# A hybrid decoder step on one core: the second chunk's first norm, the samples' pages and queries, the page-number check and the mixers' halves

## What is computed

```
x += 0.5 * SwiGLU1(RMSNorm(x))                      # 2816 hidden
z  = RMSNorm(x) @ w_in                              # q, k, v, indexer q/k/weights, conv B, C, h
       I[t,s] = sum_h w[t,h] relu(q_idx[t,h].k_idx[s]); keep top k = 256 keys (s <= t),
       softmax attention over the kept keys (8 q heads, 2 kv heads, dim 64, rotary)
       short gated conv (512 channels): y = B * conv_w3(C * h)
x += concat(attn, conv) @ w_out
x += 0.5 * SwiGLU2(RMSNorm(x))
x += sigmoid(RMSNorm(x) @ w_ple_gate) * (p @ w_ple_proj)
y  = RMSNorm(x)
```

## Time and profile before

| | before |
|---|---|
| median of 3 runs | 2928.32 us (2918.21 to 2932.49) |
| the profiled execution, its own time | 2924.44 us |
| its span, first to last instruction | 2922.7 us |
| mean granted TensorE clock | 0.943 |
| busy, share of the span | TensorE 89%, VectorE 45%, GpSimd 35%, ScalarE 34% |
| HBM | 89 GB/s over the span |

### The profile page before, as it was taken

How to read it: one execution, slowest core, us unless ns; L and a number is a source line. 1 busy time by engine, 2 the same in 40 slices (tenths; PEclk the granted TensorE clock), 3 DMA queues, 4 the chain that set the end, 5 groups by cost and what they waited for, 6 DMA issues and landing times.

```text
span 2922.7 us, 41456 instructions
## 1 busy us (share of the span) xinstructions
PE 2615.3 (89%) x15166; PEld 2282.7 (78%) x15166; DVE 1313.0 (45%) x3135; ACT 1001.1 (34%) x1625; POOL 1009.9 (35%) x521
## 2 busy tenths in 40 slices
PE   4999998998868888889898976888999999999997
PEld 4999997778646767777786676777889898778786
DVE  3223224438753333443365687766333232332344
ACT  3222223631213333335435311443444233332332
POOL 4333333232343333332244223212213344454440
PEclk9999998999878888899999988998999999999998
DMA  4333324221224343311222212111112223233212
GB/s 147 98 95 100 107 92 140 93 106 63 96 79 124 103 136 116 119 57 49 77 101 75 70 61 73 44 44 44 44 44 87 80 72 115 87 108 96 92 63 73
DMA packets 157038, 253.40 MB, mean 87 GB/s; under 512 B 15010, under 2 KB 101283, under 8 KB 156835
## 3 DMA queue, kind: packets, MB, share of 16 engines
q1 hardware_dynamic: 154144, 247.02, 26.5%
q10 hardware_dynamic: 2690, 3.72, 0.4%
HBM read 240.34 MB, written 18.73 MB: 89 GB/s over the span
## 4 chain that ended last, share of the span: by engine, by line
PE 69%; DVE 14%; ACT 4%; issue 4%; POOL 3%; DVEq 2%; DMA 1%; SPq 1%; ACTq 0%
PE ps L1442 21%; PE ps L1443 19%; PE ps L1444 19%; PE ps L1655 2%; PE ps L1711 2%; DVE hits L1242 1%; POOL w_lo L734 1%; DVE s_hits L1292 1%; DVE hits_late L1242 1%; PE ps L1641 1%; DVE ps L1092 1%; POOL d_lo L734 1%; PE ps L1577 1%; DVE ha_lo L1094 1%; SPq L613 1%
## 5 line engine op out<-in xcount | busy, mean ns | idle before, releaser
L734 POOL TENSOR_TENSOR w_lo<-raw,w_hi 128x1024 fp32r<-128x1024 f32 x250 | 602.5, 2412 | 1058.7 <-ACT w_hi L834 1058.1
L1442 PE MATMUL ps<-xna_hi,w_hi 128*128 128x288 f32 x2000 | 612.3, 306 | 29.6 <-DVE convf_a L1146 7.8
L1443 PE MATMUL ps<-xna_lo,w_hi 128*128 128x288 f32 x2000 | 600.7, 300 | 0.0
L1444 PE MATMUL ps<-xna_hi,w_lo 128*128 128x288 f32 x2000 | 599.8, 300 | 0.0
L1442 PEld LDWEIGHTS ps<-xna_hi,w_hi 128*128 128x128 f32 x2000 | 387.6, 194 | 44.6 <-issue 22.8
L1442 PE MATMUL ps<-xnb_hi,w_hi 128*128 128x512 f32 x1000 | 412.8, 413 | 0.3 <-DVE hb_lo L1094 0.3
L734 POOL TENSOR_TENSOR d_lo<-raw,d_hi 128x1024 fp32r<-128x1024 f32 x90 | 218.4, 2446 | 544.6 <-ACT d_hi L834 544.6
L1443 PE MATMUL ps<-xnb_lo,w_hi 128*128 128x512 f32 x1000 | 400.6, 401 | 0.0
L1444 PE MATMUL ps<-xnb_hi,w_lo 128*128 128x512 f32 x1000 | 400.2, 400 | 0.0
L1443 PEld LDWEIGHTS ps<-xna_lo,w_hi 128*128 128x128 f32 x2000 | 387.3, 194 | 0.2
L1444 PEld LDWEIGHTS ps<-xna_hi,w_lo 128*128 128x128 f32 x2000 | 386.5, 193 | 0.0
(11 more groups left out here) (291 smaller groups left out, 4126.8 us busy)
## 6 DMA issues: line engine op xcount, KB each, us to landing
raw<-in_w_gu SPq DMA_DIRECT2D x176, 512.0 KB, 3.5
raw<-in_w_d SPq DMA_DIRECT2D x88, 512.0 KB, 3.5
raw<-in_w_ring SPq DMA_DIRECT2D x74, 512.0 KB, 3.4
pages<-in_vk_pages SPq DMA_DIRECT2D x256, 128.0 KB, 2.7
idx_flat<-in_idx_pages SPq DMA_DIRECT2D x256, 32.0 KB, 2.1
idxp<-idx_flat SPq DMA_DIRECT2D x8, 1024.0 KB, 7.6
x_spill<-xa SPq DMA_DIRECT2D x1, 2304.0 KB, 8.9
xa<-x_spill SPq DMA_DIRECT2D x4, 576.0 KB, 5.9
```

The lines of the kernel that those rows point to most:

```text
L734: g_.tensor_tensor(lo[slot][:, :, :], raw[l % 2][:, :, :], hi[slot][:, :, :].bitcast(f32), ALU.subtract).then_inc(lo_done, 1)
L1442: mm(out, shi, mhi, start=first, stop=False)
L1443: mm(out, shi, mlo, start=False, stop=False)
L1444: return mm(out, slo, mhi, start=False, stop=last)
```

## The change

- **Start.** `weights` is cut in two: tiles 0 and 1 are split ahead of the first `sums`, tiles 2 and 3 behind the eight scales of chunk 0. Squares 0 to 3 of chunk 1 go between `sums` and `spread` of chunk 0, squares 4 to 7 between scales 3 and 4. `sums(0,1)` stands behind the first half of the first product, `spread(0,1)` and the scales of chunk 1 behind its second. The gathers are woven over a list shorter by these two parts.
- **Search and pages.** 10 search steps in the in-projection in place of 12, 22 in the feed-forward. The first three `kl` join the feed-forward's search groups 2, 4 and 6 (steps 12, 14, 16), `qs` and the first `ks` group 10 (step 20). SP's and GpSimd's wait for the mask becomes one for the in-projection's last product; ScalarE's is dropped. Search and choice steps are woven over parts 2 to 54 (2 to 50 before), the rest of the samples' work from part 55 (51). By the weave, the three choice steps then all follow the third down-projection (two of them preceded it), and four quarters lie between the last of them and the first `kq`.
- **Memory.** K pages move from FREE to XNA + 16384, the exponentials' input Sa from XNA to FREE, `above` and `cum` into the places of V pages 3 to 6; mask, scores and hits shift.
- **Page numbers** are loaded without the bounds check.
- **Mixers.** Copies and subtractions tile by tile, attn and conv alternately; TensorE waits per tile, SP for all.
- **End.** `spread(4,0)` behind the last product.

```diff
--- before.py
+++ after.py
@@ -231,9 +231,14 @@
         flat = lambda groups: [e for g in groups for e in g]
-        ev = [("begin",)] + flat(squares(0, 0)) + [("weights",)] + self.norm(0, 0) + flat(squares(0, 1)) + self.norm(0, 1)
+        scales = lambda k, c, ms: [("scale", k, c, m) for m in ms]
+        second = flat(squares(0, 1))
+        ev = [("begin",)] + flat(squares(0, 0)) + [("weights", 0), ("sums", 0, 0)] + second[:4] + [("spread", 0, 0)]
+        ev += scales(0, 0, range(4)) + second[4:] + scales(0, 0, range(4, KT)) + [("weights", 1)]
 
         first = self.two_chunks(0, range(FT))
+        ev += first[:1] + [("sums", 0, 1)] + first[1:2] + [("spread", 0, 1)] + scales(0, 1, range(KT))
+        first = first[2:]
         first = weave(first, [[("ga", i)] for i in range(NB * PAGES // 2)], 1, 140)
@@ -248,20 +253,24 @@
         side += [[("spread", 0, 2)] + [("scale", 0, 2, m) for m in range(4)], [("scale", 0, 2, m) for m in range(4, KT)], [("vtr", 0)]]
-        side += [[("st", j)] for j in range(12)]
+        side += [[("st", j)] for j in range(10)]
         ev += weave(first, side, 13, None)
         first = self.one_chunk(0)
-        search = [[("st", j)] for j in range(12, 32)] + [[("sties", i)] for i in range(3)] + [[("qs",)]]
+        search = [[("st", j)] for j in range(10, 32)] + [[("sties", i)] for i in range(3)]
         groups = self.samples()
+        for i in range(K_RING):
+            search[2 + 2 * i] += groups[i]
+        search[10] += [("qs",)] + groups[K_RING]
+        groups = groups[K_RING + 1:]
         for j in range(32):
-            groups[6 + 2 * j].append(("bt", "A", j))
+            groups[2 + 2 * j].append(("bt", "A", j))
         units = self.prompt(BLOCKS[0])
         units[6].append(("bties", 3))
-        first = weave(first, groups + units + [[], [("mix", 0)], [("back", 0)]], 51, -3)
-        ev += weave(first, search, 2, 50)
+        first = weave(first, groups + units + [[], [("mix", 0)], [("back", 0)]], 55, -2)
+        ev += weave(first, search, 2, 54)
         first = self.out_proj(0)
@@ -292,7 +301,7 @@
         end = len(first) - 4
-        ev += first[:end] + [("sums", 4, 0)] + first[end:end + 1] + [("spread", 4, 0)] + first[end + 1:]
+        ev += first[:end] + [("sums", 4, 0)] + first[end:] + [("spread", 4, 0)]
         ev += [("scale", 4, 0, m) for m in range(KT)] + [("y", 0)] + self.norm(4, 1) + [("y", 1)]
@@ -308,7 +317,7 @@
             if e[0] == "weights":
-                for w in range(RING):
+                for w in (2 * e[1], 2 * e[1] + 1):
                     split(("w", w), "w", w)
@@ -468,13 +477,13 @@
 
-        scores = {0: at("score0", [128, 128], f32, FREE + 12352), 1: at("score1", [128, 256], f32, FREE + 12864),
-                  2: at("score2", [128, 384], f32, FREE + 13888), 3: at("score3", [128, 512], f32, H + 10752),
+        scores = {0: at("score0", [128, 128], f32, FREE + 12640), 1: at("score1", [128, 256], f32, FREE + 13152),
+                  2: at("score2", [128, 384], f32, FREE + 14176), 3: at("score3", [128, 512], f32, H + 10752),
                   4: at("score4", [128, 640], f32, FREE), 5: at("score5", [128, 768], f32, FREE + 2560),
         s_hits = at("s_hits", [128, HW], bf16, FREE + 8224)
-        smask = at("smask", [128, HW], bf16, FREE + 8224)
+        smask = at("smask", [128, HW], bf16, FREE + 8448)
         idxp = [at(f"idxp{s}", [128, 4, 512], f32, XNB + 8192 * s) for s in range(2)]
@@ -482,7 +491,7 @@
         rl = [at("rl_a", [128, 2, 512], f32, XNB + 27264), at("rl_b", [128, 2, 448], f32, H)]
-        hits = {2: at("hits2", [128, 384], bf16, FREE + 6144), 3: at("hits3", [128, 512], bf16, FREE + 6912),
+        hits = {2: at("hits2", [128, 384], bf16, XNA + 22528), 3: at("hits3", [128, 512], bf16, XNA + 23296),
                 6: at("hits6", [128, 896], bf16, XNB + 25088), 7: at("hits7", [128, 1024], bf16, XNB + 26880)}
@@ -499,9 +508,9 @@
 
-        above = at("above", [128, HW], bf16, XNA + 17152)
-        cum = at("cum", [128, HW], fp16, XNA + 21280)
-        Sa = [at(f"Sa{s}", [128, 1024 + NS], f32, XNA + 16384 + 4352 * s) for s in range(2)]
+        above = at("above", [128, HW], bf16, XNA + 6144)
+        cum = at("cum", [128, HW], fp16, XNA + 10272)
+        Sa = [at(f"Sa{s}", [128, 1024 + NS * s], f32, FREE + 4096 * s) for s in range(2)]
         qs_hi, qs_lo, qs_f = [at(name, [128, 4, 192], dt, XNA + o) for name, dt, o in (("qs_hi", f32r, 25088), ("qs_lo", f32r, 28160), ("qs_f", f32, 28160))]
@@ -510,11 +519,11 @@
 
-        pages = at("pages", [128, 241, 128], f32, XNA)
-        k_tile, v_tile = (lambda n: 225 + 4 * (n % K_RING)), (lambda n: 4 * (n % V_RING))
+        pages = at("pages", [128, 4 * (V_RING + K_RING), 128], f32, XNA)
+        k_tile, v_tile = (lambda n: 4 * (V_RING + n % K_RING)), (lambda n: 4 * (n % V_RING))
         slot_of = lambda tile: pages[:, tile:tile + 4, :].rearrange("p (b r) n -> p b (r n)", b=2)
         kv_k = [slot_of(k_tile(s)) for s in range(K_RING)]
-        kv_kr = [at(f"kv_kr{s}", [128, 2, 256], f32r, FREE + 2048 * s) for s in range(K_RING)]
+        kv_kr = [at(f"kv_kr{s}", [128, 2, 256], f32r, XNA + 16384 + 2048 * s) for s in range(K_RING)]
         kv_v = [slot_of(v_tile(s)) for s in range(V_RING)]
@@ -611,7 +620,8 @@
                 return nc.values_load_multi_w_load_instructions(ptab[0:1, first:first + k], engines=(mybir.EngineType.SP,),
-                                                                min_val=0, max_val=NPOOL - 1)[1]
+                                                                min_val=0, max_val=NPOOL - 1,
+                                                                skip_runtime_bounds_check_because="a page table holds pages of the pool")[1]
 
@@ -679,7 +689,7 @@
                 if k == 0:
-                    sp.wait_ge(smask_ready, 1)
+                    sp.wait_ge(prod_done, last_in[0] + 1)
                 if k >= K_RING:
@@ -693,8 +703,8 @@
                 sp.wait_ge(x_spilled[g], 16)
-                sp.wait_ge(mixa_ready, g + 1)
-                sp.wait_ge(mixc_ready, g + 1)
+                sp.wait_ge(mixa_ready, 4 * g + 4)
+                sp.wait_ge(mixc_ready, 4 * g + 4)
                 for j in range(4):
@@ -762,7 +772,7 @@
             def sample_queries():
-                pool.wait_ge(smask_ready, 1)
+                pool.wait_ge(prod_done, last_in[0] + 1)
                 pool.wait_ge(rope_done, n("rope", T_V - 1, 0))
@@ -784,8 +794,9 @@
             def mix(g):
-                pool.wait_ge(mix_hi, 2 * g + 1)
-                g_.tensor_tensor(xn_lo[g][:, 4:8, :], convf[g][:, :, :], xn_hi[g][:, 4:8, :].bitcast(f32), ALU.subtract).then_inc(mixc_ready, 1)
+                for j in range(4):
+                    pool.wait_ge(mix_hi, 8 * g + 2 * j + 2)
+                    g_.tensor_tensor(xn_lo[g][:, 4 + j, :], convf[g][:, j, :], xn_hi[g][:, 4 + j, :].bitcast(f32), ALU.subtract).then_inc(mixc_ready, 1)
 
@@ -986,9 +997,7 @@
                 act.wait_ge(kv_loaded[s], 64 * ((k - 1) // K_RING + 1))
-                if k <= 2:
-                    act.wait_ge(smask_ready, 1)
-                else:
+                if k > 2:
                     act.wait_ge(s_mm, n("kq", *divmod(k - 3, 4)))
@@ -1017,8 +1026,9 @@
                     act.wait_ge(s_o, 4)
-                A(xn_hi[g][:, 4:8, :], convf[g][:, :, :], ACT.Copy).then_inc(mix_hi, 1)
-                A(xn_hi[g][:, 0:4, :], attn[g][:, :, :], ACT.Copy).then_inc(mix_hi, 1)
+                for j in range(4):
+                    A(xn_hi[g][:, j, :], attn[g][:, j, :], ACT.Copy).then_inc(mix_hi, 1)
+                    A(xn_hi[g][:, 4 + j, :], convf[g][:, j, :], ACT.Copy).then_inc(mix_hi, 1)
 
@@ -1421,8 +1431,9 @@
             def mix(g):
-                dve.wait_ge(mix_hi, 2 * g + 2)
-                v.tensor_tensor(xn_lo[g][:, 0:4, :], attn[g][:, :, :], xn_hi[g][:, 0:4, :].bitcast(f32), ALU.subtract).then_inc(mixa_ready, 1)
+                for j in range(4):
+                    dve.wait_ge(mix_hi, 8 * g + 2 * j + 1)
+                    v.tensor_tensor(xn_lo[g][:, j, :], attn[g][:, j, :], xn_hi[g][:, j, :].bitcast(f32), ALU.subtract).then_inc(mixa_ready, 1)
 
@@ -1436,7 +1447,7 @@
             transpose = nc.tensor.transpose
-            seen = set()
+            seen, mixed = set(), set()
 
@@ -1494,15 +1505,15 @@
                         pe.wait_ge(lo_done, plan.pos["w", w] + 1)
-                    if kind == "out" and key[0] == 0:
-                        pe.wait_ge(mixa_ready, g + 1)
-                        pe.wait_ge(mixc_ready, g + 1)
                 k = {"gate": 2 * key[0], "up": 2 * key[0], "in": 1, "out": None, "pg": 3}[kind]
                         normed(k, c, kt)
+                    elif (g, kt) not in mixed:
+                        mixed.add((g, kt))
+                        pe.wait_ge(*((mixa_ready, 4 * g + kt + 1) if kt < 4 else (mixc_ready, 4 * g + kt - 3)))
```

## The result

The changed kernel took 2884.93 us, the median of four runs (2882.45 to 2886.01), against 2926.95 for the kernel before (2918.21 to 2932.49): a ratio of 0.9859, interval 0.9842 to 0.9876, so 42 us or 1.4% less. The forecast was 2881. The profiled execution of the changed kernel took 2886.01 us, its span 2884.2, against 2922.7: 38.5 less, where the sum said 47.1. Behind the near hit stand a term that came out right, one too large, one too small by a place it had costed at nothing, and one with the wrong sign. One execution of `mix_whole`, further down, took 4176.21 us at a mean granted clock of 0.555; it was in a slower state, and its median is taken without it.

What follows compares the result with a forecast made beforehand. Outside full feed-forward stages, TensorE's waits for key low halves, sums of squares, weight copies and the mixer were taken as the bound. Terms 13 + 19 + 12 + 2.5 + 0.6 = 47.1 gave 2877.3, median 2881.2; range 2866 to 2896.

Steps and rivals of the forecast that it cites:

- Part 1: Kernel start: first low half near 24, seven products done at 55.2 instead of TensorE resuming at 68.1; 13 us, ends 9 and 16.
- Part 2: Pages and queries loaded ahead of the mask, so the key product follows it at once; 19 us, ends 11 and 22.
- it ends 12.4 us sooner: Third down-projection, with all search steps before it and the three choice steps after it, ends 12.4 us sooner.
- of which I count 1.5 us as VectorE idle: First search step starts three quarters of a product later in the in-projection; 1.5 us of that counted as VectorE idle.
- Part 3: Page numbers loaded unchecked: five places where they come last, mainly key waits and ScalarE's copies; 12 us, ends 3 and 25.
- In the gather stage the 32 batches lie beside a full TensorE: nothing: Gather stage: faster unchecked batches of eight page numbers gain nothing, as TensorE is fully busy there.
- Part 4: First mixer by tile: TensorE's 6.3 us wait for the low half shrinks; 2.5 us gained, ends 0.5 and 5.
- the exclusive port's 1.3: First mixer: if VectorE and GpSimd shut each other out, the last tile ends as before and 1.3 us is gained.
- the free tiles' 3.5: First mixer: if the tiles ran free of each other, 3.5 us would be gained.
- Part 5: Kernel end: chunk 0's last spread leaves the last product, so sigmoid and tail come sooner; 0.6 us, ends 0 and 1.
- the clock falls: Rival: samples' stage at clock 0.67 throughout, 70 us more, 2951 us; chance 0.03.
- The mask is the wall: Rival: VectorE's chain to the mask slower or its lost start not made up; about 30 us gained, 2898; chance 0.22.

Runs made afterwards that it cites:

- mix_whole: The changed kernel with the mixers' halves made whole again instead of tile by tile: 2879.24 us, median of three, ratio 0.9854.
- split_late: The changed kernel with the split of weight tiles 2 and 3 moved behind the eight scales of chunk 1: 2892.48 us, ratio 0.9886.
- nocheck_alone: The kernel before with only the bounds check of page numbers dropped: 2904.90 us against 2929.59, ratio 0.9922.
- st12: The changed kernel with twelve search steps beside the in-projection instead of ten: 2876.41 us, ratio 0.9827.
- pages12_alone: The kernel before with only the search and pages change, but its old twelve search steps beside the in-projection: 2908.30 us against 2924.36, ratio 0.9948.
- start_alone: The kernel before with only the new start: 2914.12 us against 2929.59, ratio 0.9948.

## Why the prediction came out near, point by point

Run alone, the three large parts gave 15, 8.6 and 23 us where the prediction had 13, 19 and 12. Two misses of 10 and 11 us in opposite directions cancelled; that the total came within 4 us of the forecast is in this respect luck, while its direction and the places where time was gained are not.

**Part 1, 13 us: right.** First product at 22.7 (24 forecast), seventh done near 56.7 (55.2), 12.8 us at the copy of x. The products' times lie off by a step that wasn't seen: spread(0,1) stood behind diagonals that took 4.23 us. The prediction weighed the exclusive port for the mixer, and not for the split of tiles 2 and 3 that the change puts beside the second norm. By the Trainium skill (SBUF — State Buffer, Who interferes with whom) VectorE is locked out there with two inputs from SBUF or in a two-port mode, which a `tensor_scalar` can take. The diagonals are of that kind, with one such input and a scalar; whether they ran in the mode no row shows. That the split is what holds them up `split_late` does show (4.23 to 0.68). By `nocheck_alone`, 3 us of the 13 are the SiLU wait, which either part removes alone: in a sum they may stand once, and here they do.

**Part 2, 19 us: mechanism right, size wrong, 9 to 14 measured.** Alone it gave 8.6. In the changed kernel the first key product comes 25.8 us sooner; less the 12.8 of the start, and with the quarter of 1.36 added, that is 14, but the new start alone already brings 17.6 at this place, and then 9.5 are left. Serial loading is gone as forecast, the mask and the key product are 0.5 us apart, TensorE stands 9.0 us before the mask (11 forecast). The step that failed is 'it ends 12.4 us sooner' with 'of which I count 1.5 us as VectorE idle'. Two steps fewer in the side list space out every other group in it. The index keys' loads, which wait for room, fell behind, the scales of chunk 2 met the product that reads them (6.9 us), and the search started 9.1 us later than with the new start alone (648.64 against 639.50). `st12` and `pages12_alone` show it from both sides: 8.5 and 7.5 us for the two steps by medians, 10.7 and 11.4 at the counts. With twelve, part 2 alone gave 15 to 16.

**Part 3, 12 us: right for the samples' stage, too small as a whole.** 12.4 alone, of them 7.4 from the transposed weights to the tenth, while the key waits it counted at five fell by 0.8. 'In the gather stage the 32 batches lie beside a full TensorE: nothing' is wrong by 4.3 us at the copy of x in the old kernel and by nothing in the changed one, where part 1 has paid that already. The batch behind the mask, 4.4 us alone, it had left to part 2. Undone in the changed kernel, part 3 costs 16 at the return of x and 21 to 24 by the times, more than the 12 either way.

**Part 4, 2.5 us: 2.1 at the mixer, nothing at the end.** Between the exclusive port's 1.3 and the free tiles' 3.5. The eight subtractions, GpSimd's and VectorE's:

```profile
1402.25 7.61 POOL L799 TENSOR_TENSOR xna_lo<-convf_a,xna_hi 128x576 fp32r<-128x576 f32 x4
```

```profile
1400.41 8.17 DVE L1436 TENSOR_TENSOR xna_lo<-attn_a,xna_hi 128x576 fp32r<-128x576 f32 x4 [3.13 <-ACT xna_hi L1030]
```

From GpSimd's start to its end it is 7.6 us, the 7.5 that the two engines took together before. That is what taking turns gives: the finer pieces save no time of their own, they only let TensorE start earlier. Three waits of TensorE, none above 1.2, are left. What the prediction had at nothing is the stretch behind the embeddings, 2.3 us lost on the average of the traces with the mixers by tile.

**Part 5, 0.6 us: wrong sign, a loss of 1.7.** The 0.7 for the earlier sigmoid is there. What was missed is that spread is an event of two engines: moving TensorE's six matmuls moves VectorE's diagonals behind the last addition as well, a thing that the prediction does count for other steps.

**The rest of the gap is TensorE's clock, and part of that follows from part 4.** 44.8 us stood at the embeddings, 42.1 at the first output and 38.5 at the end. The stretch between the first two has the same work and, around its middle, the same two waits, 3.7 and 3.7 us before, 4.0 and 3.7 after. Windows around them, before and after, the granted clock being the third figure from the end:

```profile
2770.00:2780.00 10.00, 8.20 (x41) 8.23 (x42) 2.49 (x5) 4.58 (x8) 3.98 (x2) 0.66 0.33 106
2780.00:2790.00 10.00, 6.26 (x37) 6.03 (x36) 7.62 (x12) 4.37 (x8) 4.90 (x4) 0.83 0.17 54
```

```profile
2725.00:2735.00 10.00, 7.63 (x33) 7.66 (x34) 2.49 (x5) 4.95 (x7) 4.55 (x2) 0.53 0.33 105
2735.00:2745.00 10.00, 6.26 (x31) 6.03 (x31) 5.57 (x10) 2.58 (x4) 2.88 (x2) 0.67 0.19 54
```

TensorE came back to full speed later, and 2.6 us went there and 1.5 in the last product. Two windows at the same place of `mix_whole`, from the start of GpSimd's split of those two tiles:

```profile
2723.09:2733.09 10.00, 7.50 (x36) 7.53 (x37) 2.49 (x5) 5.07 (x7) 4.68 (x2) 0.66 0.36 107
2733.09:2743.09 10.00, 6.26 (x37) 6.03 (x36) 6.92 (x12) 3.88 (x7) 4.20 (x3) 0.83 0.20 54
```

The 2.6 are thus no accident of one execution: a wait of 4.0 us in place of 3.7, and the clock behind it at 0.53 and 0.67 in place of 0.66 and 0.83. The 1.5 in the last product did vary: without the old end's spread the last two sums stand 7.02 or 8.5 us apart, in two and three traces. `nocheck_alone` lost 5.7 us behind the embeddings' load as well, `start_alone` none. The rival 'the clock falls' was put at 70 us and a whole stage; nothing like it happened, but differences of 2 to 10 us between executions of like work did, and they are as large as the smaller terms of the sum.

None of the four rivals happened. 'The mask is the wall' came nearest: VectorE's start was lost as it has it, and part 2 alone, with 8.6 us, lies nearer to its 6 than to the forecast's 19. Part 3, where it had 8, kept the total away from it.
